# A two-block network on one core: expert loads start during the output projections, attention works by two heads, and the last output tile and the token squares come in pieces

## The reference

```python
h = rmsnorm(x, norm1_g) * (1.0 + sc1) + sh1
q_m, k_m, v_m, q_d, k_d, v_d, gate_m, gate_d = split(h @ w_in)
o_m = moba_attention(rope(q_m), rope(k_m), v_m)      # 8 heads of 64
o_d = diff_attention(rope(q_d), rope(k_d), v_d, lam) # 4 heads, 2 components each, values of 128
o_d = rmsnorm(o_d, subln_g) * (1.0 - lam_init)
merged = sigmoid(gate_m) * (o_m @ w_proj_moba) + sigmoid(gate_d) * (o_d @ w_proj_diff)
x = x + g1 * (merged @ w_out)
h2 = rmsnorm(x, norm2_g) * (1.0 + sc2) + sh2
# top group of 4, top 2 of its 8 experts, each expert 1024 -> 512 -> 1024
x = x + g2 * sum_over_chosen(w * (silu(h2 @ w_gate[e]) * (h2 @ w_up[e])) @ w_down[e])
return rmsnorm(x, final_g)
```

## Time and profile before

| | before |
|---|---|
| median of the runs | 1378.05 us |
| the profiled execution's own time | 1381.08 us |
| its span, first to last instruction | 1378.5 us |
| TensorE busy | 1337.0 us (97%) |
| VectorE busy | 639.5 us (46%) |
| ScalarE busy | 267.1 us (19%) |
| read from HBM | 348.82 MB, 254 GB/s over the span |
| mean granted TensorE clock | 0.992 |

### The profile page before, as it was taken

One profiled execution on the slowest core, in us unless ns is written; L12 is line 12 of the kernel. 1 busy time (PEld: TensorE's weight loads), 2 busy tenths in 40 slices (PEclk: granted clock), 3 DMA queues, 4 the chain that ended last, 5 costly groups with the idle time before them and its releaser, 6 DMA issues.

```text
span 1378.5 us, 18034 instructions
## 1 busy us (share of the span) xinstructions
PE 1337.0 (97%) x6780; PEld 925.9 (67%) x6780; DVE 639.5 (46%) x1349; ACT 267.1 (19%) x542; POOL 45.9 (3%) x47
## 2 busy tenths in 40 slices
PE   8999999999999999999999999999999999999997
PEld 6888888888888888888784788854333433334332
DVE  4552389998325777611531455244332333323323
ACT  2311133210103000000442331034111111112111
POOL 0001002000000111100000000000000000000000
PEclk9999999999999999999999999999999999999999
DMA  7354333334447889758434233199999999999994
GB/s 264 122 174 132 122 123 122 123 122 155 151 142 277 311 292 318 235 156 318 175 141 165 80 122 123 61 371 416 427 428 429 396 419 428 428 429 428 427 428 196
DMA packets 118879, 350.71 MB, mean 254 GB/s; under 512 B 4385, under 2 KB 66081, under 8 KB 106273
## 3 DMA queue, kind: packets, MB, share of 16 engines
q1 hardware_dynamic: 117200, 348.68, 66.1%
q10 hardware_dynamic: 1616, 1.20, 0.3%
HBM read 348.82 MB, written 1.05 MB: 254 GB/s over the span
## 4 chain that ended last, share of the span: by engine, by line
PE 83%; DMA 12%; DVE 2%; issue 1%; ACT 1%; SPq 0%; POOL 0%; DVEq 0%; POOLq 0%; ACTq 0%
PE bank L666 45%; PE bank L1049 16%; DMA arena<-in_w_up 6%; DMA dense<-in_w_gate 6%; PE bank L868 6%; PE bank L939 4%; PE bank L1021 2%; PE bank L883 2%; PE bank L1121 2%; PE bank L814 1%; PE bank L897 1%; PE bank L779 1%; PE bank L705 1%; PE bank L924 0%; PE bank L720 0%
## 5 line engine op out<-in xcount | busy, mean ns | idle before, releaser
L666 PE MATMUL bank<-hT,dense 128*128 128x256 f32 x2112 | 459.9, 380 | 1.9 <-ACT hT L1182 1.1
L666 PEld LDWEIGHTS bank<-hT,dense 128*128 128x128 f32 x2112 | 400.0, 190 | 64.1 <-issue 9.3
L1049 PE MATMUL bank<-arena,scratch 128*64 128x512 f32 x768 | 171.4, 599 | 8.4 <-DMA arena<-in_w_up 5.7
L666 PE MATMUL bank<-arena,dense 128*128 128x256 f32 x768 | 167.4, 380 | 0.0
L666 PEld LDWEIGHTS bank<-arena,dense 128*128 128x128 f32 x768 | 145.8, 190 | 21.0 <-issue 1.2
L1049 PEld LDWEIGHTS bank<-arena,scratch 128*64 128x64 f32 x768 | 58.1, 138 | 113.7 <-issue 113.4
L1049 PE MATMUL bank<-arena,hT 128*64 128x512 f32 x512 | 113.4, 595 | 0.7 <-ACT hT L1423 0.7
L1624 DVE SCALAR_TENSOR_TENSOR arena<-arena,par 128x256 f32<-128x256 f32 x240 | 97.8, 485 | 0.0
L2041 DVE TENSOR_TENSOR scratch<-scratch,bank 128x512 f32<-128x512 f32 x64 | 41.2, 683 | 97.9 <-PE bank L1121 96.4
L1049 PEld LDWEIGHTS bank<-arena,hT 128*64 128x64 f32 x512 | 35.3, 137 | 66.5 <-issue 64.0
L868 PE MATMUL bank<-region,dense 128*128 128x256 f32 x352 | 76.1, 379 | 0.0
(11 more groups left out here) (322 smaller groups left out, 1082.9 us busy)
## 6 DMA issues: line engine op xcount, KB each, us to landing
arena<-in_w_up SPq DMA_DIRECT2D x32, 2048.0 KB, 17.2
arena<-in_w_down SPq DMA_DIRECT2D x30, 2048.0 KB, 16.5
dense<-in_w_in SPq DMA_DIRECT2D x24, 2048.0 KB, 8.2
dense<-in_w_gate SPq DMA_DIRECT2D x16, 2048.0 KB, 22.8
arena<-in_w_gate SPq DMA_DIRECT2D x14, 2048.0 KB, 23.3
arena<-in_w_ada SPq DMA_DIRECT2D x12, 2048.0 KB, 7.7
dense<-in_w_ffn_up SPq DMA_DIRECT2D x22, 1024.0 KB, 7.0
dense<-in_w_ffn_down SPq DMA_DIRECT2D x8, 1408.0 KB, 7.1
```

The lines of the kernel that those rows point to most:

```text
L666: last = mm(dst, chunk(k, m), src[:, k, :], start=k == 0, stop=k == k_n - 1)
L1049: last = mm(dst[e * CAP:(e + 1) * CAP, :], tokens(k, e), w[e][:, k, :], start=k == 0, stop=k == k_n - 1)
```

## The change

- **Early expert loads.** The down weights of pair 0's first expert go to `region[:, 0:4096]` (`first_down`), which `qk` held, once the attention's last squares are summed (`ossq_done`). `gates2` moves to slot 5 whole, so that slot 4 is free when proj_d is done: it takes the down weights of pair 1's first expert behind the load of out2's second unit. The gate weights of pair 1 for the dense slot with out2's first unit are issued after out2's tile 1. After tile 3 two loads are left (down of pair 0's second expert, the other gate). `first_refill` then loads one down tile instead of two. The first `down` reads `first_down`.
- **Attention.** The first query block sees only the first 128 keys: scores, mask, exponentials and scaling take 384 columns instead of 512, with a reduction and a scaling for each block. For the eight heads of 64, the value products of two heads are issued together after the odd one, the two heads alternating.
- **Last output tile.** The second chunk of tile 3 goes to the free half of tile 1's bank; between the two chunks TensorE does the transposes and logits of chunks 4 and 5, and then 6 and 7 one by one.
- **Squares and rows.** Squares are summed in three pieces for each block (512, 256, 256 columns), and the rows are copied to `r_tok` (`scratch1`) directly, without the later copy from `x_rows`. `scale_rows` reads `r_tok` and waits for the first pair's down. `g2_diag` moves to `hT`.
- **Routing.** The first selection matrices take two instructions of 256 columns instead of four of 64. TensorE issues one more unused matmul behind the ranking.

The diff, without the moves of buffers and counters:

```diff
+        at[0] = 5 * SLOT
...
+        SEEN = T + P
+        seen = (slice(T, SEEN), slice(0, T))
...
+        first_down = region[:, 0:SLOT]
...
+            sp.wait_ge(sem_("ossq_done"), 1)
+            load_expert(first_down, down_in[0], wde, 0, 0)
             stage("out2", 2, flat, lambda u: wo2[:, :, ds(u * 512, 512)])
-            wait_all_read(sp, "out2")
-            load_downs(0)
+            sp.wait_ge(down_in[0], 16)
+            load_expert(down_slot[0], down_in[0], wde, 0, 1)
+            first = U0("out2") % 2
+            sp.wait_ge(tile_done, TILE["out2", 1] + 1)
+            load_expert(gate_slot[1][first], gate_in[1][first], wge, first, 1)
             sp.wait_ge(tile_done, TILE["out2", 3] + 1)
-            load_gates(1, 1)
+            load_expert(down_slot[1], down_in[1], wde, 1, 0)
+            load_expert(gate_slot[1][1 - first], gate_in[1][1 - first], wge, 1 - first, 1)
...
-                load_downs(1)
+                load_expert(down_slot[1], down_in[1], wde, 1, 1)
...
-                        o, b = m * 64, v3(bank[4 + m][:], T)
-                        last = mm(b[:, c, :], qk[o:o + 64, j, c * P:(c + 1) * P], qk[o:o + 64, j + 4, :],
-                                  start=True, stop=True)
+                        o = m * 64
+                        last = mm(bank[4 + m][:, seen[c]], qk[o:o + 64, j, c * P:(c + 1) * P],
+                                  qk[o:o + 64, j + 4, 0:(c + 1) * P], start=True, stop=True)
...
+                if a < 8 and a % 2 == 0:
+                    return
                 pe.wait_ge(sem_("prT_ready"), n + 1)
-                p = prT[:, n % 2, :]
-                o, w, vv, hh = ((a % 2) * 64, 64, vm, a) if a < 8 else (0, P, vd, n - 8)
-                if a == 0:
+                if a == 1:
                     wait_all_read(pe, "v")
-                elif a < 8 and a % 2 == 0:
+                elif a < 8:
                     pe.wait_ge(sem_("o_read"), a // 2)
-                elif a >= 8:
+                else:
                     pe.wait_ge(sem_("o_read"), n - 4)
-                mm(bank[7][o:o + w, 0:T], vv[:, 0, hh * w:(hh + 1) * w], p[:, 0:T], start=True, stop=False)
-                mm(bank[7][o:o + w, P:T], vv[:, 1, hh * w:(hh + 1) * w], p[:, T:T + P], start=False,
-                   stop=True).then_inc(sem_("o_done"), 1)
+                w, vv, hs = (64, vm, (a - 1, a)) if a < 8 else (P, vd, (n - 8,))
+                for late in range(2):
+                    for i, h in enumerate(hs):
+                        p = prT[:, (h if a < 8 else n) % 2, :]
+                        last = mm(bank[7][i * w:(i + 1) * w, late * P:T], vv[:, late, h * w:(h + 1) * w],
+                                  p[:, T:T + P] if late else p[:, 0:T], start=not late, stop=late == 1)
+                last.then_inc(sem_("o_done"), 1)
...
-            out2_tile(3)
-            route_pair(2)
-            route_pair(3)
+            out2_tile(3, half=sem_("first_half"), between=lambda: route_pair(2), second=out2_bank[1][:, T:2 * T])
+            pe.wait_ge(sem_("lg_bias"), 2)
+            pe.wait_ge(sem_("rows_read"), 4)
+            route((6,))
+            wait_read(pe, TILE["out2", 3])
+            route((7,))
...
+            keep_on(bank[5], 1)
...
+                slots = [first_down, down_slot[1]] if very_first else down_slot
...
+            for q in range(2):
+                act.wait_ge(sem_("turned"), 2 + q)
+                for c in range(TT):
+                    square(c, q, 2 * q + c + 1)
+                    copy_rows(c, q)
+            act.wait_ge(sem_("turned"), 5)
+            square(0, 2, 5)
...
-                    own.do(f(x_rows[:, c, :], x_rows[:, c, :], ACT.Copy, scale=rsum[:, c:c + 1]))
+                    own.do(f(x_rows[:, c, :], r_tok[:, c, :], ACT.Copy, scale=rsum[:, c:c + 1]))
...
-                    act.wait_ge(sem_("rows_read"), 4)
-                    for c in range(TT):
-                        f(r_tok[:, c, :], x_rows[:, c, :], ACT.Copy).then_inc(sem_("sum_opened"), 1)
                 pair(0, v)
                 if b == 0:
-                    act.wait_ge(sem_("sum_opened"), TT)
+                    act.wait_ge(sem_("rows_read"), 6)
+                    act.wait_ge(sem_("down_used"), 1)
...
-                stt(srow[:, r, :], bank[4 + r][:], 0.125, con("att_mask"), ALU.mult, ALU.add).then_inc(sem_("masked"), 1)
+                stt(srow[:, r, 0:SEEN], bank[4 + r][:, 0:SEEN], 0.125, con("att_mask")[:, 0:SEEN], ALU.mult, ALU.add
+                    ).then_inc(sem_("masked"), 1)
                 dve.wait_ge(sem_("masked"), a + 1)
-                do(V.tensor_reduce(mx[:, 2 * r:2 * r + 2], v3(srow[:, r, :], T), AX_X, ALU.max))
+                for c in range(TT):
+                    do(V.tensor_reduce(mx[:, 2 * r + c:2 * r + c + 1], srow[:, r, seen[c]], AX_X, ALU.max))
...
-                    ins = tt(pr, pr, rsum[:, 2 * r:2 * r + 2].unsqueeze(2).to_broadcast([P, TT, T]), ALU.mult)
-                    if a < 8:
-                        ins.then_inc(sem_("prob_ready"), 1)
-                    else:
-                        do(ins)
+                    for c in range(TT):
+                        pr = prob[:, r, seen[c]]
+                        ins = ts(pr, pr, rsum[:, 2 * r + c:2 * r + c + 1], None, ALU.mult)
+                        if c == 1 and a < 8:
+                            ins.then_inc(sem_("prob_ready"), 1)
+                        else:
+                            do(ins)
...
+            dve.wait_ge(sem_("first_half"), 2)
+            add_branch(6, bank[TILE["out2", 3] % NB][:, 0:T]).then_inc(sem_("lg_bias"), 1)
+            wait_tile(dve, "out2", 3)
+            add_branch(7, bank[TILE["out2", 1] % NB][:, T:2 * T]).then_inc(read_sem("out2", 3), 1)
...
-                    for n, (o, col) in enumerate(places):
-                        ins = ts(sel[:, r, o:o + CAP], con("slot"), rank[:, ds(col, 1)], rsum[:, n // 2:n // 2 + 1],
-                                 ALU.is_equal, ALU.mult)
-                        own.do(ins) if n < 3 or r else ins.then_inc(sem_("sel_ready"), 1)
+                    at_slot = sel[:, r, :].rearrange("p (c e s) -> p c e s", c=TT, e=2)
+                    slot = con("slot").unsqueeze(1).unsqueeze(1).to_broadcast([P, TT, 2, CAP])
+                    place = v3(rank[:], E_)[:, :, 2 * r:2 * r + 2].unsqueeze(3).to_broadcast([P, TT, 2, CAP])
+                    own.do(tt(at_slot, slot, place, ALU.is_equal))
+                    scale = rsum[:, 0:TT].unsqueeze(2).to_broadcast([P, TT, 2 * CAP])
+                    ins = tt(v3(sel[:, r, :], 2 * CAP), v3(sel[:, r, :], 2 * CAP), scale, ALU.mult)
+                    own.do(ins) if r else ins.then_inc(sem_("sel_ready"), 1)
```

## The result

| | before | changed |
|---|---|---|
| median of seven runs each | 1382.87 us (1377.29 to 1385.02) | 1372.66 us (1371.54 to 1375.91) |
| ratio, 95% interval | | 0.9937 (0.9916 to 0.9957) |
| profiled execution: time, span | 1381.08, 1378.5 us | 1371.54, 1369.7 us |
| TensorE busy | 1337.0 us | 1326.5 us |
| mean granted clock | 0.992 | 0.996 |

The forecast was 9.7 us less, a ratio of 0.9930 to the 1378.05 that was known then. The measured ratio is 8.7 us of 1378.05 (5.9 to 11.6 by its interval), the two medians are 10.2 us apart, and the two profiled spans 8.8. The forecast absolute time, 1368.4, was missed by 4.3 us, because it started from a low median: the first three runs of the kernel before gave 1378.05, all seven give 1382.87.

A forecast was written before the change was run, and what follows sets the result against it. The end was bound by the expert-load stream: its start, bytes left and holes; TensorE set the pace before it. 6.4 + 4.9 + 0.9 - 3.8 + 1.3 = 9.7 us off 1378.05 gave 1368.4 us, range 1364.5 to 1374.

The forecast's parts named there:

- rival 1: Expert stage: the room from early loads is given back as holes move, leaving 1372.6 us; chance 0.14.
- Attention: Attention heads: fewer score columns save 2.1 us, paired value products 3.2, VectorE adds no wait; -5.3 us (-1.2 to -5.7).
- Last output tile: Tile 3 of the output: shorter copy and square on VectorE, but last transposes some 0.4 us later; -0.1 us.
- Gather's clock and the count: Before the first gate: filler keeps the gather's clock up, but the count's register load, taken as 0.6 us, leaves 0.5 us.
- s = 6.4: Everything ahead of the experts: TensorE reaches them 6.4 us earlier, 5.3 plus 1.1 (range 1.8 to 7.4).
- One tile less, earlier resume, new holes: Expert stream from the first refill: 2.1 MB less to move -4.9 us, resuming earlier -0.9, holes without backlog +3.8.
- The dip at 1100: Where the refill order changes and the queue ran dry: half of the 2.65 us lost there goes, -1.3 us.
- The stream, -3.3: Expert loads together: one tile less -4.9 us, earlier resume -0.9, new holes +3.8, smaller dip at the order change -1.3.
- rival 3: Better than counted: order-change hole goes wholly, count's load free, clock stays up; 12 us off, 1365 us; chance 0.13.
- Rival 2: Attention: paired heads' value products don't overlap in the array, 2.7 us less gained, 1371.1 us; chance 0.08.
- rival 4: Attention: VectorE's more and smaller instructions become the bound, 15 us of TensorE waits, 1383 us; chance 0.03.
- rival 5: Early expert loads don't run early because SP holds them behind a wait; given no chance of its own.

The follow-up runs named there:

- a3: The changed kernel with the count of the fullest expert written ahead of the routing weights; 1372.59 us, ratio 0.9935.
- d3: The changed kernel with one head's value products issued wholly after the other's, not alternating; one profile, 1376.40 us.
- a1: The changed kernel with SyncE's order of expert loads put back as before; 1375.11 us, ratio 0.9953.
- c2: c1 with SyncE's early expert loads undone; 1374.24 us, ratio 0.9938.
- c1: The changed kernel with the refill order changed in two steps: for pairs 5 and 6 one gate tile ahead of the ups, one behind; 1370.82 us, ratio 0.9916.
- d1: c1 with the count written early and, for pairs 5 and 6, the second gate tile behind the downs; 1367.27 us, ratio 0.9891.
- a4: The changed kernel with the count written early and the refill order changed at pair 9 instead of 7; 1371.72 us, ratio 0.9929.

## Why the prediction was right or wrong, step by step

The direction held, and the sum was off by 0.9 us: 9.7 forecast, 8.8 between the profiles, 8.7 by the ratio. The terms err more than the sum, so that closeness is in part luck. Two steps failed. The load of the count was put at 0.6 us and took its whole 1.13, so the clock gained in the gather brought nothing; and the dip at the change of order was to shrink by 1.3 us and did not shrink. A third effect, 1.7 us from the clock at the sums of squares, was put at nothing because it was not looked for; it about made up for both. The time itself, 1368.4, also missed because of the median that it was taken from. That the 1372.66 measured lies on rival 1's 1372.6 is chance: the kernel before had moved by 4.8 us.

- **Attention, -5.3**: the sums' start moved from 834.62 to 829.93, and the attention's own start had come 0.32 us later (752.32 to 752.64), so -5.0. No run undid the attention alone; this stands on the profiles. The overlap, the scores and VectorE's chain (2.31 us for the 2.37 estimated, no wait) came as worked out; only a set of scores costs 0.85 us, for the 0.80 forecast.
- **The clock at the sums, no term, -1.7**: I had costed only one fall, at the gather, and not looked at the other idle time of 1.9 us in the same stretch; the trace of before had that fall too, so "this trace has one such fall" was wrong.
- **Last output tile, -0.1**: measured +0.3 (from its first matmul to the logits 890.08 to 900.78 before, 883.71 to 894.73 now: 10.70 and 11.02). "TensorE issues the same work" was true, but four small groups of one chunk each take longer than one group of two.
- **Selection, -0.5**: measured -0.6.
- **Gather's clock and the count, -0.5**: measured 0. This step failed. I set the register load at 0.6 us out of a bound of 0 to 1.13, and so let the clock gain through. The load's whole 1.13 us were there, in both kernels: the gate's start followed the count by exactly that. The profile's releaser, ScalarE, was wrong both times; a3 shows it.
- **s = 6.4** was thus measured as 6.6, by errors that cancel: 1.7 not seen, against 0.5 (count), 0.4 (tile) and 0.3 (attention) too much, and 0.3 by which the attention started later.
- **One tile less, earlier resume, new holes, -4.9 - 0.9 + 3.8**: the holes came where forecast, 4.5 us more than before by the slices for the 3.8 counted. That would leave 1.3 us; the span shows 2.2, and the slices are too coarse to settle the rest. (The 2 us from issue to flow don't follow from the row named for them, 7.7 - 4.9 = 2.8; in the changed profile, 114 GB/s over the 2.3 us behind the first refill, some 1.7 us went by.)
- **The dip at 1100, -1.3**: measured 0 (3.4 us lost before, 3.3 now). This is the other step that failed, and the one with a lesson. I took the dip for a shortage that shrinks when TensorE has waited less. It is where the order of the loads changes with all slots full; its length follows TensorE's own lateness (5.3 us by the slices in a3 and 4.7 in d3, where the group ahead of it ran slow), and behind it the program takes 278.6 to 278.9 us where the last gate runs at full clock, and 279.4 to 280.3 where it doesn't, whatever came before. So bytes loaded early count there only as far as they bring TensorE to it sooner.
- **The stream, -3.3** in all: -2.2 in the first pair of profiles (-1.4 on the average of all, by the start of the group ahead of the switch), -2.4 by a1's runs. Rival 1 (the room is given back) had the right mechanism for the difference, at about a quarter of its price (1.1 of 4.3 us by the first pair); with the dip softened the loads are worth 3.4 us (c2 against c1), which the runs can't tell from 2.4.
- **Rival 2** (no overlap), **rival 4** (VectorE binds) are refuted by the rows above, and so is **rival 5**: the early loads ran early. Of **rival 3** one part came true (the clock stayed up in the gather) and one in part (one wait of 2.2 us fewer in the stage); the load of the count was not free, and the dip went only in d1.
- The predicted pace of the late pairs (29.4 us) held: 1273.18 to 1302.41 and 1331.79, the starts of their gates, are 29.2 and 29.4 us apart.

## What to carry to other kernels

A stream that is the bound on the average is not the bound everywhere: look for the last point at which its queue runs dry and waits for an engine, for all that is gained ahead of it counts only as far as it brings that engine there sooner. When the order of loads has to change, change it by one tile at a time; here that gave 4.4 us over moving the point of change by two pairs (d1 against a4, both with the count early), which had given nothing by itself. Where a group runs fast in one execution and slow in the next, compare several profiles, at a point ahead of it or with it alike: one pair said 2.2 us for the early loads and next to nothing for the count, more of them 1.4 and 1.9. And where a wait's named releaser has a constant distance to some other event over several profiles (1.13 us here), believe the distance, and test it by moving that event.

## What the runs showed of the hardware that I had not expected

- The granted clock is a matter of the execution. After the same wait of 2.1 us the same 32 records took 7.09 us at 1193.75 and 8.78 at 1223.13 in the first profile of before, and 8.78 at 1193.69 in the second (the last gate of before, after 2.04, 2.71 and 2.03 us: 7.09, 8.69, 7.09). But one place was constant per kernel: the sums, slow in three of three profiles of before, fast in thirteen of thirteen of changed kernels, with 1.90 us of idle time each. Why is open. The Trainium skill (TensorE: Matmul & The Clock Gate, Part 1: The HAM clock gate) says that the point of change moves from run to run; the last gate agrees, and so does the later fall at the sums in the second profile of before, but not that the changed kernels never had it.
- When TensorE waits for a count, 1.13 us pass from the end of VectorE's write to the first matmul behind the register load (what part of it is the load, no view shows), and nothing that can be seen when the count is written ahead of a gather that is still being worked off (a3: gate behind gather without a gap).
- Two products with weights of 64 columns in different halves of the array overlap in whichever order their four matmuls are issued (0.80 us alternating, 0.81 one head after the other, 0.79 for one head alone).
